# When the sample attention's keys are loaded and its first steps start, in a one-layer hybrid decoder step

## The chip, the cores and the metric

The kernel runs on one core of a Trainium2 chip. The metric is the device time in microseconds of one execution, lower is better. Before the change it was 835.45 us, the median of three executions (833.49 to 836.05).

## The reference

One decoder layer is computed for two groups of tokens with the same weights: a prompt of 256 tokens and 8 sample sequences of 8 tokens, whose keys and values of 256 past tokens lie in a paged cache. Cut to what matters:

```python
h = rmsnorm(x, norm1_g)
proj = h @ w_in                        # 12 sections; the attention takes fq, fk, fv and the gates ff
h_a = mlstm_sequence(q_a, k_a, v_a, ig, lf_a, C, n, m)      # matrix memory, one branch
q_b, k_b = rmsnorm(fq, q_norm_g), rmsnorm(fk, k_norm_g)     # per head of 128
k_all = concatenate([k_past, k_b]); v_all = concatenate([v_past, fv])
F_all = cumsum(concatenate([lf_past, lf_b]))
s = q_b @ k_all.T / sqrt(128) + F_q - F_k                   # causal
o_b = softmax(s) @ v_all                                    # forgetting attention, other branch
x = x + (sigmoid(ga) * (h_a @ w_branch_mlstm) + sigmoid(gb) * (o_b @ w_branch_fox)) @ w_out
x = x + hierarchical_moe(rmsnorm(x, norm2_g), ...)          # 32 experts, top 1 group, top 2 in it
```

For the samples b = 0 to 7 the attention has 8 heads, 8 queries and 256 past plus 8 new keys each.

## The kernel before

The dense weights come in 48 chunks of 256 columns, four for each of the twelve sections (mo, mk, mq, mv, ga, gb, fk, fq, fv, bm, bf, out). SyncE (SP) loads a chunk of 1 MB, ScalarE (ACT) rounds it to a high part (L829) and VectorE (DVE) subtracts to get the low part (L1172), and TensorE (PE) multiplies it in two or three units. In sections such as fv, units 0 and 1 are the two prompt tiles of 128 tokens and unit 2 the 64 sample tokens (L1811, 16 matmuls); unit 2 is evacuated by an ACT copy (L849) and a DVE addition (L1534, semaphore low_added). In bm a chunk has two units of 24 matmuls (L1821). Unit (fv,3,2) is unit 2 of chunk 3 of fv, the last of that section.

Between units every engine runs small stages in an order fixed by the function stages(): each entry names a unit behind which the stages stand, and each engine walks the same table in order and takes the stages that it has work for. Engines wait for each other only through semaphores, and each runs its own instructions strictly in that order.

For the samples a pipeline of stages runs, one step n after each unit from (fv,2,2), step 0, over (fv,3,1), step 1, (fv,3,2), step 2, and (bm,0,0), step 3, to step 9. For sample b:

- FS0(b), on DVE only: three copies (L1466, L1467, L1471) lay the new keys, the queries and the past forget values where PE reads them, then semaphore fs_ready. In step b-1; FS0(0) stands alone, behind unit (fv,2,1).
- FS1(b), in step b: PE waits for fs_ready and for the past keys (keys_landed) and computes scores (L2032, L2037, L2040). DVE takes the maximum (L1478 to L1480), ACT the exponential (L1041), DVE normalises.
- FS2(b), in step b+1: PE transposes the probabilities (L2049) and DVE lays them out (L1497, L1498).
- FS3(b), in step b+2: PE multiplies by the values: 24 matmuls of 128x128, 48 records in the trace (L2067), in three groups j: j = 0 and 1 are the two pages of past values, j = 2 the new ones, which lie in fv. In FS3(0) alone PE waits, ahead of group j = 2, until all of fv is evacuated.
- FS4(b), also in step b+2: a transpose into the output of the attention.

In each step PE runs FS3, FS2, FS1, then stages FP3, FP2, FP1 of the prompt's attention (L2013 is in FP2), then FS4.

GpSimd (POOL) issues the loads of past keys and values on its own queue, in a fixed order. Each sample needs two DMAs of 512 KB for keys (L664) and two for values (L679), and each time it first reads two page numbers. keys(b) goes to a first buffer for b = 0 and odd b, to a second for b = 2, 4, 6; the second lies on an area that PE reads as the dense input up to unit (fv,3,1) (unit (fv,3,2) reads another copy of the samples' part). keys(2) waits until that unit is done; the others wait until PE is past FS1(b-2), keys(1) past FS1(0). values(b) has two buffers in turn and waits from b = 2 on until PE is past FS3(b-2). The order of issue is values 0, keys 1, values 1, keys 2, keys 3, values 2, keys 4, the two stores of the new v rows (L641), values 3, keys 5, values 4, keys 6, values 5, keys 7, values 6, values 7.

After the attention come the sections bm, bf and out, the router, and the 32 experts, whose 96 MB of weights SP streams through buffers as they come free; the first wait of that stream behind the router is for its split input.

Of the kernel before, what the change touches and what calls it, by code (L numbers as in the profile page):

```python
# [30 lines left out]
TP, BS, TS = 256, 8, 8  # L31
# [6 lines left out]
HF, DF = 8, 128  # L38
# [10 lines left out]
CPS = D // CW  # L49
# [18 lines left out]
def units_of(c):  # L68

    return 2 if SECTIONS[c // CPS] in BY_FEATURE else 3  # L70


def stages():

    order = [(c, u) for c in range(NCH) for u in range(units_of(c))]
    at = {cu: [] for cu in order}

    def after(section, chunk, unit, n=0):

        return at[order[order.index((CPS * SECTIONS.index(section) + chunk, unit)) + n]]  # L80

    for n in range(1, 6):
        after("mo", 0, 1, 1 + 3 * (n - 1)).append(("G", n, 0))
    for t in range(3):
        after("mq", 1 + t, 1).append(("KT", t, 0))

    for h in range(HM):
        after("mv", h, 2, 2 if h < HM - 1 else 1).append(("P2", 0, h))
        after("mv", h, 2).append(("P1", 0, h))
    after("ga", 0, 0).append(("F1", 0, 0))  # L90
    for h in range(HM):
        after("ga", 1, 1, h).append(("P2", 1, h))
        after("ga", 0, 1, h).append(("P1", 1, h))
    after("ga", 0, 1).append(("F3", 0, 0))
    after("ga", 1, 0).append(("F2", 0, 0))

    after("ga", 2, 1).append(("SA", 0, 0))
    after("ga", 3, 0).append(("F1", 1, 0))
    for h in range(HM):
        for b in range(BS):  # L100
            line = after("ga", 3, 1, (h * BS + b) * 9 // (HM * BS))
            line.append(("SB", h, b))
            if h == 0 and b in (4, 5, 6):
                line.extend({4: (("F2H", 1, 0),), 5: (("F2L", 1, 0), ("F2H", 1, 1)), 6: (("F2L", 1, 1),)}[b])
        if h < HM - 1:
            line.append(("SA", h + 1, 0))
    after("ga", 3, 1).append(("F3", 1, 0))
    after("fk", 0, 0).append(("F1", 2, 0))
    after("fk", 0, 1).append(("F3", 2, 0))
    after("fk", 1, 0).append(("F2", 2, 0))  # L110

    for w, section in enumerate(("fk", "fq")):
        for t in range(3):
            after(section, 3, 2, 2 * t).append(("N1", w, t))
            after(section, 3, 2, 2 * t + 3).append(("N2", w, t))

    after("fv", 2, 1).append(("FS0", 0, 0))
    for n in range(HF + 2):
        line = after("fv", 3, 0, n) if n else after("fv", 2, 2)
        line.extend((k, n - s, 0) for s, k in ((2, "FS3"), (1, "FS2"), (0, "FS1"), (-1, "FS0")) if 0 <= n - s < BS)  # L120
        line.extend((k, n - s, 0) for s, k in ((2, "FP3"), (1, "FP2"), (0, "FP1")) if 0 <= n - s < HF)
        if n >= 2:
            line.append(("FS4", n - 2, 0))
    return at
# [32 lines left out]
def hybrid_step(nc, A, O):  # L157

    AT = stages()
    fill, count = {}, {b: 0 for b in range(8)}  # L160
    for c in range(NCH):
# [6 lines left out]
    with ctx:  # L168
        handles = {}

        def sem(name):
            if name not in handles:
                
                handles[name] = ctx.enter_context(nc.semaphore(name))
            return handles[name]
# [22 lines left out]
        def take(n):  # L198
            top[0] += n
            assert top[0] <= FW, top[0]  # L200
            return fm[:, top[0] - n:top[0]]

        def cube(ap, a):
            return ap.rearrange("p (a b) -> p a b", a=a)
# [5 lines left out]
        upto, last, maskT, mask, after = take(128), take(128), take(128), take(128), take(128)  # L210
# [62 lines left out]
        fv = cube(take(3 * D), 3)  # L273
# [116 lines left out]
        def keys_of(b):  # L390

            return KTc[1 if b >= 2 and b % 2 == 0 else 0]

        def keys_landed(b):

            other = b >= 2 and b % 2 == 0
            return sem("other_keys_in" if other else "keys_in"), 16 * NPAGES * (b // 2 if other else BS + 1 + (b + 1) // 2)

        def of_head(ap, h):

            n = HF // 2
            at = DIAGQ * n * (h // n) + HQ * (h % n)
            return ap[:, at:at + HQ]

        def units(c):

            return sum(units_of(k) for k in range(c)), units_of(c)

        def n_low(c):

            return sum(units_of(k) == 3 for k in range(c))
# [5 lines left out]
        def first(section):  # L417

            return CPS * SECTIONS.index(section)
# [157 lines left out]
        def _(pool):  # L577
# [57 lines left out]
            def pe_past(st):  # L635

                b = banks_of(st)[-1]
                pool.wait_ge(sem(f"bank_full{b}"), fill[st, b] + 1)

            def out(dst, src, name):  # L640
                pool.dma_start(dst, src).then_inc(sem(name), 16)  # L641
# [10 lines left out]
            def pages(b):  # L652

                return [pool.value_load(pt[0:1, b * NPAGES + j:b * NPAGES + j + 1], min_val=0, max_val=NPHYS - 1)
                        for j in range(NPAGES)]

            def keys(b):

                if b == 2:
                    pool.wait_ge(sem("unit_full"), units(first("bm"))[0] - 1)  # L660
                elif b:
                    pe_past(("FS1", max(b - 2, 0), 0))
                for j, page in enumerate(pages(b)):
                    pool.dma_start(keys_of(b)[:, :, j * PAGE:(j + 1) * PAGE],  # L664
                                   A["cache_kT"][bass.ds(page, 1)].rearrange("a d h s -> (a d) h s"))\
                        .then_inc(keys_landed(b)[0], 16)
# [7 lines left out]
            def values(b):  # L674

                if b >= 2:
                    pe_past(("FS3", b - 2, 0))
                for j, page in enumerate(pages(b)):
                    pool.dma_start(Vc[b % 2][:, j, :], A["cache_v"][bass.ds(page, 1)].rearrange("a s f -> (a s) f"))\  # L679
                        .then_inc(sem(f"values_in{b % 2}"), 16)  # L680
# [28 lines left out]
            g(nc.gpsimd.memset(qms, 0.0))  # L709
            g(nc.gpsimd.memset(Ps[0:NS, :], 0.0), sem("att_zeroed"))  # L710
            values(0)
            keys(1)
            values(1)
            keys(2)
            keys(3)
            for b in range(2, BS):
                if b == 3:

                    pool.wait_ge(sem("unit_free_a"), units(first("bm"))[0] - n_low(first("bm")))
                    pool.wait_ge(sem("low_added"), n_low(first("bm")))  # L720
                    out(O["v_prompt"], fv[:, 0:2, :], "v_stored")
                    out(O["v_sample"], fv[0:NS, 2, :], "v_stored")
                values(b)
                if b + 2 < BS:
                    keys(b + 2)

            pool.wait_ge(sem("o_split"), KC)
            g(nc.gpsimd.iota(iota, pattern=[[1, SLOTS]], base=0, channel_multiplier=0,
# [79 lines left out]
        def _(act):  # L808
# [108 lines left out]
            def P1(st):  # L917
                _, c, h = st
                n = c * HM + h
                if n == 0:  # L920
                    act.wait_ge(sem("gate_acts"), 2)
                if n >= 2:
                    pe_past(("P2", (n - 2) // HM, (n - 2) % HM))
                s(A_(kw[n % 2], kM(c, h), ACT.Copy, scale=ew[:, c, 8 + h:9 + h]), sem("kw_ready"))
# [848 lines left out]
        def _(pe):  # L1773
# [3 lines left out]
            def claim(st, b):  # L1777

                if fill[st, b]:
                    pe.wait_ge(sem(f"bank_free{b}"), fill[st, b])  # L1780

            def full(ins, b):
                ins.then_inc(sem(f"bank_full{b}"), 1)
# [268 lines left out]

            def FS3(st):
                b = st[1]
                pe.wait_ge(sem("fs_pt"), b + 1)
                pe.wait_ge(sem(f"values_in{b % 2}"), 16 * NPAGES * (b // 2 + 1))
                claim(st, 4)
                for j in range(3):
                    if b == 0 and j == 2:

                        pe.wait_ge(sem("unit_free_a"), units(first("fv") + CPS)[0] - n_low(first("fv") + CPS))
                        pe.wait_ge(sem("low_added"), n_low(first("fv") + CPS))
                    for h in range(HF // 2):
                        for i in range(2):
                            g = h + HF // 2 * i
                            w = slice(DF * g, DF * (g + 1))
                            ins = mm(bank[4][HQ * i:HQ * (i + 1), 0:DF], of_head(PTm[:, j, :], g),  # L2067
                                     Vc[b % 2][:, j, w] if j < 2 else fv[:, 2, w],
                                     start=(h == 0 and j == 0), stop=(h == HF // 2 - 1 and j == 2),
                                     skip_group_check=True)  # L2070
                full(ins, 4)
# [265 lines left out]
```

## Time and profile before

| | |
|---|---|
| median of 3 executions | 835.45 us (833.49 to 836.05) |
| profiled execution, its own time | 833.49 us |
| its span | 832.0 us |
| PE busy | 739.5 us, 89% |
| DVE busy | 401.7 us, 48% |
| ACT busy | 298.4 us, 36% |
| POOL busy | 140.0 us, 17% |
| read / written | 184.24 MB / 23.12 MB |

The span is the time from the first to the last instruction of the profile; the execution's own time is 1.5 us longer. PE is the tensor engine's matmuls and PEld its weight loads. An fp32 matmul shows as two records. A line of a timeline gives the start in us from the span's start, the duration, the engine, the line of the kernel, the operation with its output and inputs, and in brackets how long the engine was idle ahead of it and who released it; "issue" means that the profile shows no instruction as the releaser, and a wait for a load appears so. DMAs issued by POOL are timed at the issue; the time to landing is given apart.

### The profile page before, as it was taken

Reading aid. Unit: us, or ns where it says so; the run is one execution under the profiler, and the core shown is the slowest. Engines: PE = TensorE matmul, PEld = TensorE weight load, DVE = VectorE, ACT = ScalarE, POOL = GpSimd, SP = SyncE. Lnnn points to the kernel's source line nnn. Section 1 sums busy time; section 2 is a strip of 40 time slices with the busy share of each in tenths; the row PEclk is TensorE's granted clock in tenths of the full one; section 3 lists DMA queues with packets and bytes.
Section 4 is the critical chain, followed back from the end, with each engine's and each line's share of the span. In section 5 each row is a group of like instructions: output and inputs, shape, how many; then the busy total and the mean of one; then the engine's idle time right before and its main releaser. Section 6 shows DMA issues by size and latency. Waiting matters only on the chain.

```text
span 832.0 us, 14577 instructions
## 1 busy us (share of the span) xinstructions
PE 739.5 (89%) x5478; PEld 592.1 (71%) x5478; DVE 401.7 (48%) x939; ACT 298.4 (36%) x550; POOL 140.0 (17%) x247
## 2 busy tenths in 40 slices
PE   2999999999999999999899999895899999778770
PEld 1899999998666698998678889884665555344430
DVE  3466233465755556575566657755732222121123
ACT  5532644374543354555322234545221111111110
POOL 5001000001444200232312101000012222211210
PEclk9999999999999999999999999997899999999995
DMA  5344333224888643636776337965599999999985
GB/s 193 102 153 147 139 127 132 102 102 163 256 254 243 214 148 113 216 111 216 239 262 231 110 117 294 343 269 215 224 415 416 419 418 418 419 420 418 420 338 201
DMA packets 38186, 202.58 MB, mean 243 GB/s; under 512 B 7442, under 2 KB 7970, under 8 KB 18914
## 3 DMA queue, kind: packets, MB, share of 16 engines
q1 hardware_dynamic: 23938, 158.98, 49.4%
q0 software_dynamic: 13744, 41.32, 15.6%
q10 hardware_dynamic: 432, 1.31, 0.4%
q8 instruction: 46, 0.75, 0.4%
q14 instruction: 26, 0.21, 0.1%
HBM read 184.24 MB, written 23.12 MB: 249 GB/s over the span
## 4 chain that ended last, share of the span: by engine, by line
PE 64%; DMA 16%; DVE 10%; ACT 5%; issue 4%; SPq 0%; DVEq 0%; ACTq 0%; POOLq 0%
PE bank L1821 22%; PE bank L1825 12%; DMA fm<-in_w_moe 10%; PE bank L2183 7%; PE bank L1811 4%; DMA em<-in_w_moe 3%; PE bank L2203 3%; PE bank L1983 3%; DVE rm L1172 2%; ACT rm L829 2%; PE bank L2155 2%; PE bank L1972 2%; PE bank L2067 1%; DMA fm<-y_rows 1%; PE bank L2032 1%
## 5 line engine op out<-in xcount | busy, mean ns | idle before, releaser
L1821 PE MATMUL bank<-rm 128*128 128x320 f32 x1344 | 207.3, 313 | 1.6 <-ACT fm L857 1.6
L1821 PEld LDWEIGHTS bank<-rm 128*128 128x128 f32 x1344 | 198.9, 189 | 5.7 <-issue 3.1
L1172 DVE TENSOR_TENSOR rm<-fm,rm 128x2048 fp32r<-128x2048 f32 x48 | 110.0, 2292 | 72.1 <-ACT rm L829 71.5
L1825 PE MATMUL bank<-rm 128*128 128x256 f32 x960 | 123.8, 289 | 2.4 <-DVE fm L1563 2.4
L1825 PEld LDWEIGHTS bank<-rm 128*128 128x128 f32 x960 | 119.9, 196 | 3.3 <-issue 2.9
L2183 PE MATMUL bank<-fm,em 128*64 128x256 f32 x368 | 90.9, 392 | 16.6 <-DMA fm<-in_w_moe 11.2
L829 ACT ACTIVATE rm<-fm 128x2048 fp32r<-128x2048 f32 x48 | 91.9, 1915 | 17.1 <-PE bank L1821 10.9
L2183 PEld LDWEIGHTS bank<-fm,em 128*64 128x64 f32 x368 | 48.6, 140 | 51.6 <-issue 29.6
L2185 PE MATMUL bank<-fm,em 128*64 128x256 f32 x320 | 76.9, 384 | 0.0
L1130 ACT ACTIVATE fm<-bank 64x256 f32<-64x256 f32 x32 | 12.0, 376 | 137.5 <-PE bank L2185 137.5
L761 POOL DMA_INDIRECT y_rows<-fm,im x32 | 28.9, 903 | 166.5 <-DVE fm L1718 166.5
L2185 PE MATMUL bank<-em 128*64 128x256 f32 x192 | 50.6, 411 | 0.0
L684 POOL DMA_DIRECT2D fm<-in_state_C x32 | 17.6, 550 | 164.6 <-DVE fm L1325 119.4
L1811 PE MATMUL bank<-rm 128*128 128x256 f32 x320 | 42.9, 287 | 0.0
L1404 DVE SCALAR_TENSOR_TENSOR fm<-fm,bank 128x257 f32<-128x257 f32 x64 | 28.0, 479 | 30.2 <-PE bank L1983 30.0
L1723 DVE TENSOR_TENSOR fm<-bank,fm 64x256 f32<-64x256 f32 x32 | 13.6, 426 | 59.9 <-ACT fm L1130 59.8
L1739 DVE COPY fm<-bank 128x128 f32<-128x128 f32 x32 | 9.3, 291 | 66.6 <-PE bank L2194 66.5
L2185 PEld LDWEIGHTS bank<-fm,em 128*64 128x64 f32 x320 | 41.3, 137 | 0.0
L2183 PE MATMUL bank<-em 128*64 128x256 f32 x144 | 36.0, 395 | 5.8 <-DMA em<-in_w_moe 5.8
L1811 PEld LDWEIGHTS bank<-rm 128*128 128x128 f32 x320 | 40.0, 192 | 1.6 <-DVE fm L1563 1.5
L2203 PE MATMUL bank<-em,fm 128*64 128x512 f32 x144 | 34.0, 593 | 1.5 <-issue 0.9
L1718 DVE COPY fm<-bank 64x512 f32<-64x512 f32 x32 | 22.2, 694 | 26.9 <-PE bank L2203 26.8
(399 smaller groups left out, 986.1 us busy)
## 6 DMA issues: line engine op xcount, KB each, us to landing
fm<-in_w_moe SPq DMA_DIRECT2D x57, 1024.0 KB, 23.2
fm<-in_w_dense SPq DMA_DIRECT2D x48, 1024.0 KB, 4.9
em<-in_w_moe SPq DMA_DIRECT2D x39, 1024.0 KB, 27.1
fm<-in_state_C POOLq DMA_DIRECT2D x32, 257.0 KB, 5.4
out_C_sample<-fm POOLq DMA_DIRECT2D x32, 257.0 KB, 6.5
fm<-in_cache_v POOLq DMA_DIRECT2D x16, 512.0 KB, 4.9
fm<-in_cache_kT POOLq DMA_DIRECT2D x10, 512.0 KB, 7.5
em<-in_cache_kT POOLq DMA_DIRECT2D x6, 512.0 KB, 6.0
```

The costliest lines, as they stand in the source:

```text
L761: pool.indirect_dma_start(y_rows, bass.IndirectOffsetOnAxis(ap=row_i[:, v:v + 1].bitcast(U32), axis=0), yrow[v % NY], None, bounds_check=6 ...
L829: s(A_(pair[c % 2][0], cube(raw[c % RAW1], KC), ACT.Copy), sem("hi_done"))
L1172: s(TT(pair[c % 2][1], cube(raw[c % RAW1], KC), pair[c % 2][0], ALU.subtract), sem("split_done"))
L1404: done(STT(Cout[n % NCOUT][:, k, :], Cin[n % NCIN][:, k, :], dec8[:, HM * b + h:HM * b + h + 1], bank[bk][:, 0:DE], ALU.mult, ALU.add), bk)
L1718: CP(yrow[v % NY][:, D // 2:D], bank[4 + v % 2][CAP:2 * CAP, :]).then_inc(sem("e_y_right"), 1)
L1811: ins = mm(bank[b][:, 0:CW], samp[:, k, :], w[:, k, :], start=(k == 0 and i == 0), stop=(k == KC - 1 and i == 1))
L1821: ins = mm(bank[b][:, 0:NT], w[:, k, P * u:P * (u + 1)], a[:, k, :], start=first, stop=final)
L1825: ins = mm(bank[b][0:r, 0:CW], a[:, k, TILE0[u]:TILE0[u] + r], w[:, k, :], start=first, stop=final)
L1983: full(mm(bank[bk][:, 0:DE], kwm[n % 2][rows, 0:P], vx2[rows, h, :], start=True, stop=True), bk)
L2183: last_g = mm(bank[b][0:CAP, 0:FE], x[:, k, :], g[:, k, :], start=(k == 0), stop=(k == KC - 1), skip_group_check=True)
L2185: last_u = mm(bank[b][CAP:2 * CAP, 0:FE], x[:, k, :], u[:, k, :], start=(k == 0), stop=(k == KC - 1), skip_group_check=True)
L2203: ins = mm(bank[b][CAP * j:CAP * (j + 1), :], hT[:, k, :], w[:, k, 512 * j:512 * (j + 1)], start=(k == 0), stop=(k == 1), skip_group_check ...
```

## The change

There are three edits.

1. In stages(), FS0(0) stands behind unit (fv,2,2) instead of (fv,2,1). It is now the first stage of step 0, behind DVE's evacuation of that unit.
2. On POOL, the order of issue becomes values 0, keys 1, values 1, keys 2, values 2, the two stores of v, keys 3, values 3, keys 4, values 4 and so on to keys 7, values 7: each sample's keys right ahead of its values. keys(2) waits for the last unit of fv instead of the last but one. The buffers and the other waits stay.
3. On PE, FS3(0) waits for all of fv ahead of its first matmul instead of ahead of group j = 2, and the loops over heads h and groups j change places in FS3 of all samples, with the same matmuls.

```diff
--- before.py
+++ after.py
@@ -114,7 +114,7 @@
             after(section, 3, 2, 2 * t).append(("N1", w, t))
             after(section, 3, 2, 2 * t + 3).append(("N2", w, t))
 
-    after("fv", 2, 1).append(("FS0", 0, 0))
+    after("fv", 2, 2).append(("FS0", 0, 0))
     for n in range(HF + 2):
         line = after("fv", 3, 0, n) if n else after("fv", 2, 2)
         line.extend((k, n - s, 0) for s, k in ((2, "FS3"), (1, "FS2"), (0, "FS1"), (-1, "FS0")) if 0 <= n - s < BS)
@@ -657,7 +657,7 @@
             def keys(b):
 
                 if b == 2:
-                    pool.wait_ge(sem("unit_full"), units(first("bm"))[0] - 1)
+                    pool.wait_ge(sem("unit_full"), units(first("bm"))[0])
                 elif b:
                     pe_past(("FS1", max(b - 2, 0), 0))
                 for j, page in enumerate(pages(b)):
@@ -709,20 +709,15 @@
             g(nc.gpsimd.memset(qms, 0.0))
             g(nc.gpsimd.memset(Ps[0:NS, :], 0.0), sem("att_zeroed"))
             values(0)
-            keys(1)
-            values(1)
-            keys(2)
-            keys(3)
-            for b in range(2, BS):
+            for b in range(1, BS):
                 if b == 3:
 
                     pool.wait_ge(sem("unit_free_a"), units(first("bm"))[0] - n_low(first("bm")))
                     pool.wait_ge(sem("low_added"), n_low(first("bm")))
                     out(O["v_prompt"], fv[:, 0:2, :], "v_stored")
                     out(O["v_sample"], fv[0:NS, 2, :], "v_stored")
+                keys(b)
                 values(b)
-                if b + 2 < BS:
-                    keys(b + 2)
 
             pool.wait_ge(sem("o_split"), KC)
             g(nc.gpsimd.iota(iota, pattern=[[1, SLOTS]], base=0, channel_multiplier=0,
@@ -2052,15 +2047,15 @@
 
             def FS3(st):
                 b = st[1]
+                if b == 0:
+
+                    pe.wait_ge(sem("unit_free_a"), units(first("fv") + CPS)[0] - n_low(first("fv") + CPS))
+                    pe.wait_ge(sem("low_added"), n_low(first("fv") + CPS))
                 pe.wait_ge(sem("fs_pt"), b + 1)
                 pe.wait_ge(sem(f"values_in{b % 2}"), 16 * NPAGES * (b // 2 + 1))
                 claim(st, 4)
-                for j in range(3):
-                    if b == 0 and j == 2:
-
-                        pe.wait_ge(sem("unit_free_a"), units(first("fv") + CPS)[0] - n_low(first("fv") + CPS))
-                        pe.wait_ge(sem("low_added"), n_low(first("fv") + CPS))
-                    for h in range(HF // 2):
+                for h in range(HF // 2):
+                    for j in range(3):
                         for i in range(2):
                             g = h + HF // 2 * i
                             w = slice(DF * g, DF * (g + 1))
```

## Rows read from the trace of the kernel before

**Rows 1.** The page, busy us (share of the span) and instructions of each engine.
```profile
PE 739.5 (89%) x5478; PEld 592.1 (71%) x5478; DVE 401.7 (48%) x939; ACT 298.4 (36%) x550; POOL 140.0 (17%) x247
```

**Rows 2.** Chain of waits, 380 to 410 us: start us, duration us, what.
```profile
386.93 1.28 ACT L1041
...
396.19 2.30 DVE rm L1172
```

**Rows 3.** Timeline of PE: start us, us, engine line operation, count [idle before <-releaser].
```profile
383.15 1.97 PE L2032 MATMUL bank<-fm 128*32 128x264 f32 x16
...
387.31 6.00 PE L1825 MATMUL bank<-rm 128*128 128x256 f32 x48
...
395.09 1.97 PE L2032 MATMUL bank<-fm 128*32 128x264 f32 x16 [1.46 <-issue]
...
401.20 2.15 PE L1811 MATMUL bank<-rm 128*128 128x256 f32 x16
...
407.67 1.07 PE L2067 MATMUL bank<-fm 128*32 128x128 f32 x16 [1.68 <-DVE fm L1534]
...
408.99 1.97 PE L2032 MATMUL bank<-em,fm 128*32 128x264 f32 x16
...
421.31 1.98 PE L2032 MATMUL bank<-fm 128*32 128x264 f32 x16
...
425.80 0.52 PE L2013 MATMUL bank<-fm 128*128 128x128 f32 x3 [0.97 <-DVE fm L1498]
...
457.80 2.81 PE L2067 MATMUL bank<-fm 128*32 128x128 f32 x48
...
473.16 1.97 PE L2032 MATMUL bank<-fm 128*32 128x264 f32 x16
```

**Rows 4.** Timeline of DVE around FS0(0) and the evacuation of unit (fv,2,2).
```profile
381.31 0.19 DVE L1466 COPY fm<-fm 128x64 f32<-128x64 f32 x1
...
381.77 0.23 DVE L1471 COPY fm<-fm 128x128 f32<-128x128 f32 x1
383.79 0.42 DVE L1534 TENSOR_TENSOR fm<-bank,fm 64x256 f32<-64x256 f32 x1 [1.79 <-ACT fm L849]
```

**Rows 5.** Timeline of POOL: loads of keys and values, stores of v.
```profile
389.66 0.95 POOL L664 DMA_DIRECT2D fm<-in_cache_kT  x1 [1.16 <-issue]
...
395.06 1.79 POOL L664 DMA_DIRECT2D em<-in_cache_kT  x2 [2.54 <-issue]
...
410.81 1.15 POOL L679 DMA_DIRECT2D fm<-in_cache_v  x2 [9.55 <-issue]
413.44 1.79 POOL L664 DMA_DIRECT2D em<-in_cache_kT  x2 [1.47 <-issue]
415.22 0.57 POOL L641 DMA_DIRECT2D out_v_prompt<-fm  x1
...
462.39 1.15 POOL L679 DMA_DIRECT2D fm<-in_cache_v  x2 [8.98 <-issue]
```

**Rows 6.** Landing: all loads of line 664, then those issued from 399 to 403.
```profile
DMA to landing us min/median/max: 5.2/6.6/8.8
...
fm<-in_cache_kT POOLq DMA_DIRECT2D x2, 512.0 KB, 8.3
```

**Rows 7.** PE behind a gap; then busy time by stretch (PE, PEld, DVE, ACT, POOL, PEclk, DMA share, GB/s).
```profile
89.94 1.30 PE L1821 MATMUL bank<-rm 128*128 128x320 f32 x6 [1.58 <-ACT fm L857]
...
91.00:94.00 3.00, 3.00 (x13) 3.00 (x13) 1.59 (x1) 1.74 (x2) 0.00 (x0) 0.50 0.00 0
...
401.00:414.55 13.55, 11.17 (x122) 9.22 (x120) 6.20 (x28) 3.73 (x16) 2.48 (x5) 1.00 0.63 207
```

**Rows 8.** Busy time by stretch around the start of the expert weights' stream.
```profile
580.00:600.00 20.00, 16.59 (x100) 13.41 (x100) 15.91 (x40) 5.39 (x10) 1.23 (x2) 0.77 0.52 195
...
582.00:587.00 5.00, 3.10 (x12) 2.85 (x13) 4.68 (x10) 0.00 (x0) 0.00 (x0) 0.50 0.00 0
...
600.00:640.00 40.00, 39.40 (x287) 23.29 (x288) 14.77 (x39) 6.96 (x15) 7.69 (x10) 1.00 1.01 416
```

## The prediction

> **What bounds the kernel now.** I read the page first: the tensor engine (PE) is busy 89% of the span [rows 1], so a microsecond of PE idle time is dear unless something else sets that stretch. Then the chain of waits over the stretch that the edit touches, 380 to 480 us. From 386 to 407 us the chain runs through VectorE (DVE) and ScalarE (ACT), not PE: the exponential's table load and a weight split stand in it [rows 2]. So in steps 0 to 2 of the sample attention, PE waits on DVE, and what matters is when PE hands FS1(0) to DVE and when DVE hands the last value columns back. Then PE's timeline [rows 3], DVE's [rows 4] and GpSimd's (POOL) [rows 5], to see how long before its use each load of keys is issued, and how long loads take to land [rows 6].
>
> **Edit 1: FS0(0) one unit later.** FS0(0) is three DVE copies. Now they run from 381.31 to 382.00, beside PE's matmuls, and FS1(0) starts at 383.15 the moment PE gets there [rows 3, 4]. After the edit they stand behind the evacuation of unit (fv,2,2), whose last operation on DVE ends at 383.79 + 0.42 = 384.21. Three copies with gaps are 0.69, so they end at 384.93, and PE starts FS1(0) at about 385.0 instead of 383.15: +1.85. Nothing hides it: the chain enters DVE right behind FS1(0) [rows 2]. The first load of keys(1), released by FS1(0), moves along with it; PE's wait for it (1.46 us, at 395.09) lies beside the DVE chain and costs nothing on its own. Everything up to 407.67, where PE is released by the last value columns [rows 3], slides by 1.85.
>
> **Edit 2: FS3(0) waits for the value columns before its first matmul.** Now 32 of its 48 records run before that wait. All 48 take 2.81 us in step 6, the 16 behind the wait 1.07 [rows 3]. So 2.81 - 1.07 = 1.74 us leave the cover of the wait and stand behind it: +1.74. The wait's release is not later for it, since DVE needs nothing of FS3(0) before. Queued behind the waiting instruction are FS2(1), FS1(2) and PE's whole next unit. The loops' new order (h outside, j inside) issues the same 48 records with the same tiles. I take 0. Their spacing is now (2.81 - 1.07)/32 = 54.4 ns, and 128 columns at 2.4 GHz are 53.3, so at most 8 x 48 x 1.1 ns = 0.4 us could be gained; I allow as much for a loss.
>
> **Edit 3: the loads of keys are issued later.** keys(2) is released by the last unit of fv, not the last but one. Now it is issued at 395.06, 1.75 us after the unit that ends at 387.31 + 6.00 = 393.31, for a use at 408.99: 14 us ahead. After: the unit of 401.20 + 2.15 = 403.35 ends at 405.20 (with edit 1), the first DMA starts 1.8 later at 407.0, the second 0.9 later at 407.9 [rows 3, 5]. Landing: the second of keys(1) started at 389.66 and PE went on at 395.09, 5.4 us. The extremes of all sixteen are 5.2 and 8.8, and 8.3 is the median of keys(3), which had two other transfers ahead of it [rows 6]. keys(2) now has the queue to itself, so I take 5.4 to 6.5: landed at 413.3 to 414.4. PE, with edits 1 and 2, would reach FS1(2) at 408.99 + 1.85 + 1.74 = 412.6. The wait is 0.7 to 1.8, I take 1.1.
> The Trainium skill (DMA: Bandwidth & Descriptors, section on the SWDGE path) fits one such DMA as 2.0 us plus bytes at 436 per ns; for the 1 MB pair that would be an estimate of 4.4 us and no wait at all. The trace's 5.4 is for the same transfer and decides.
> keys(3) to keys(7) now stand behind values(b-1), which waits for FS3(b-3). For b = 3: values(2) is issued 2.07 us after FS3(0) ends (408.74 to 410.81), takes 1.15, then come the two stores of v (2 x 0.57) and two page reads (1.5, as between 411.96, the end of values(2), and 413.44), then two DMAs 0.9 apart (1.79 for two): the second starts 6.7 us after FS3(0)'s end. With 1.25 MB of stores ahead of it I take 7.4 to land: 14.1 us. FS1(3) now starts 421.31 - 408.74 = 12.6 after FS3(0); with step 2's added wait (1.1 to 1.7) 14.0, and 0.97 us of PE's wait for DVE at 425.80 can take up more. I put 0.5 on it, between 0 (landing 6.6) and 1.5 (landing 8.8). For b = 7: FS3(4) ends at 457.80 + 2.81 = 460.61, values(6) go out at 462.39, the second DMA of keys(7) at 465.9, landed with the median 6.6 at 472.5, and the need is at 473.16 [rows 3, 5, 6]. So 0.7 us spare; b = 4 to 6 follow the same pattern. I take 0 for b = 4 to 7. Key loads move past values and the stores only; SP's queue is not touched; it waits for the stores of v only in chunk 3 of bf, more than a section later.
>
> **The clock.** PE's idle time in step 2 becomes one gap: from 403.35 to 407.67 it had the 32 other records of FS3(0) in it, and now it is empty, 4.3 us. In this trace a gap of 1.58 before 89.94 was followed by a granted clock of 0.50 (1.2 GHz) from 91 to 94 with PE fully busy, while 1.68 here was not (1.00 over 401 to 414.55, 2.4 GHz) [rows 7]. So I expect the clock to fall around FS3(0). A fall as long as the one at 91 to 94, 3 us or a little more, takes half of its length, up to 1.7 us, from FS3(0) and FS2(1) [rows 7], side by side with the landing of keys(2): together they cost the later of the two, 1.7 instead of 1.1.
> The Trainium skill (TensorE: Matmul & The Clock Gate, section on the HAM clock gate) has half rate as the resting state that activity lifts; by that alone the short gap at FS1(0) is harmless, by the trace's 1.58 it may not be.
> A fall there would slow FS1(0) itself, on the chain, by up to 1.7; I leave it to the range.
>
> **Sum.** 1.85 + 1.74 + 1.7 + 0.5 = 5.8 us. Does it reach the end? From 600 us the DMA engines are saturated (share 1.01, 416 GB/s), but just ahead, 582 to 587, they move nothing and wait for the router's result [rows 8], which hangs on PE and DVE. So the weight stream starts 5.8 later and ends 5.8 later. The profiled execution took 833.49 (span 832.0 and 1.5 around it), so it gives 839.3; the median of the runs shown, 835.45, is 1.96 above the profiled one, so the forecast in its terms is 841.2.
>
> **Rivals.**
> Keys late in every step (0.10). The spare time of b = 4 to 7 is under 1 us at the median landing; at the 8.8 us seen once, keys(7) lands at 474.7, 1.5 late. Five such steps are 7.5: 835.45 + 5.3 + 7.5 = 848.3. For it speaks that values and keys now go out back to back; against it the median of 6.6.
> Step 2's load and clock both hidden (0.12): the clock stays up and keys(2) land in under 4.7. Only edits 1 and 2 remain: 3.6, so 839.0.
> Not slower, by the router's clock (0.09). Between 580 and 600 the granted clock is 0.77 [rows 8], so for 46% of 20 us, 9.2 us, PE works at 1.2 GHz, and it is on the path for most of them. Whether it falls there hangs on how PE's short waits ahead of it lie in time, and these all move. Kept up, it gives back up to 4.6: 841.2 - 4.6 = 836.6, no change, and 834.4 with the case before. Against it: the waits are the router's own and stay as long. It decides if the clock stays at 1.00 there.
> The end takes it up (0.06): if the expert weights were already flowing without a break when the delay arrives, 835.5. Against it are the 5 us at 0.00 share.
> The forecast keeps 0.63, with its own range 838.5 to 843.5.
>
> **Range and chances.** 837.0 to 846.0 leaves out about 0.10 above and 0.08 below. Such a kernel's measurement can't tell less than about 0.3% (2.5 us) from nothing. Forecast, late keys and the hidden case are all over that: slower 0.85. The other two hold 0.15: same 0.11, faster 0.04 (the router's clock together with hidden loads).
>
> **What would show it.** FS1(0) on PE starting about 1.8 later than DVE allowed before, with PE idle ahead of it, and released by DVE's third copy; one gap of some 4.3 us ahead of 48 records of FS3(0) in one piece; a lower granted clock right behind; a short wait of FS1(2) for a DMA; the second DMA of keys(b) starting 5 to 7 us after FS3(b-3). The forecast is wrong if FS1(3) to FS1(7) each wait for a DMA, or if PE reaches the unit (bm,0,0) less than 3 us later than now, or if the stretch from there to the end has another length.

## The result, and the profile after

The changed kernel took 844.9 us in the median of four runs (843.1 to 845.64), the kernel before 834.47 beside it. The ratio is 1.012, with a 95% interval of 1.0094 to 1.0148: about 10 us slower. The forecast was 841.2, in a range of 837.0 to 846.0. The profiled execution took 841.31 us, 7.8 more than the profiled one of before. Medians here leave out one execution of the kernel "order only" below, at 864.62 us, whose granted clock was 0.843 where its others had 0.965 to 0.972.

PE's timeline of the changed kernel, with the columns of [rows 3] (its lines are numbered 5 lower, and FS1 is L2027, FS3 L2062):
```profile
381.28 2.08 PE L1806 MATMUL bank<-rm 128*128 128x256 f32 x16
385.12 1.98 PE L2027 MATMUL bank<-fm 128*32 128x264 f32 x16 [1.76 <-DVE fm L1466]
...
397.45 1.98 PE L2027 MATMUL bank<-fm 128*32 128x264 f32 x16 [1.86 <-issue]
...
403.17 2.15 PE L1806 MATMUL bank<-rm 128*128 128x256 f32 x16
409.84 4.48 PE L2062 MATMUL bank<-fm 128*32 128x128 f32 x48 [4.52 <-DVE fm L1529]
...
414.57 1.97 PE L2027 MATMUL bank<-em,fm 128*32 128x264 f32 x16
...
429.60 1.98 PE L2027 MATMUL bank<-fm 128*32 128x264 f32 x16 [2.65 <-DMA fm<-in_cache_kT]
...
480.32 1.97 PE L2027 MATMUL bank<-fm 128*32 128x264 f32 x16
```
The reader is to see four places. PE idles 1.76 us ahead of FS1(0), released by DVE's third copy. Ahead of FS3(0) there is one gap of 4.52, and then its 48 records take 4.48 instead of 2.81. FS1(2), at 414.57, waits for nothing. FS1(3) waits 2.65 for keys(3), where it waited for nothing in [rows 3]. The granted clock fell at FS3(0) (columns as in [rows 7]):
```profile
405.00:409.00 4.00, 0.31 (x3) 0.11 (x1) 2.45 (x10) 1.47 (x5) 1.79 (x2) 1.00 0.08 13
409.00:412.00 3.00, 2.16 (x27) 2.19 (x29) 0.70 (x2) 0.00 (x0) 0.00 (x0) 0.74 0.94 284
```

Where a profile's early stages ran a little faster or slower, everything behind is shifted. So I count from the start of PE's unit (fv,2,2), the row at 381.28, and compare with before, where that unit started here:
```profile
381.14 2.08 PE L1811 MATMUL bank<-rm 128*128 128x256 f32 x16
```
FS1(0) at 385.12 - 381.28 = 3.84 against 383.15 - 381.14 = 2.01 is +1.83. The same sum gives +5.44 at FS1(2), +8.15 at FS1(3) and +7.02 at FS1(7); from there to the end it is +0.5.

The chain of waits of the changed kernel in steps 2 and 3 (start us, duration us, what):
```profile
409.32 0.43 DVE fm L1529
409.75 0.09 issue
409.84 4.50 PE bank L2062 x48
414.36 0.29 POOLq L654
...
416.69 0.54 POOL fm L679
417.23 0.54 POOL out_v_prompt L641
...
420.07 0.85 issue
420.93 8.58 DMA fm<-in_cache_kT
429.51 0.09 issue
429.60 1.98 PE bank L2027 x16
```
This is the new wait in one view: FS3(0) releases values(2), the stores of v follow, then keys(3), and FS1(3) waits for their landing. In the kernel before, nothing of POOL's queue stands in this chain from 380 to 430 us.

### The profile page after: what moved, and what is told of

The parts are those of the page before. It is cut to its first block, busy times and chain, and to the rows that moved or that the text cites. A ratio compares the mean times of both kernels' runs of the same rounds, so it can differ in the third digit from the quotient of the medians.

```text
span 839.7 us, 14577 instructions
## 1 busy us (share of the span) xinstructions
PE 737.7 (88%) x5478; PEld 589.1 (70%) x5478; DVE 403.3 (48%) x939; ACT 298.4 (36%) x550; POOL 140.2 (17%) x247
## 4 chain that ended last, share of the span: by engine, by line
PE 59%; DMA 17%; DVE 12%; ACT 5%; issue 5%; POOLq 0%; POOL 0%; SPq 0%; DVEq 0%; ACTq 0%
PE bank L1816 21%; DMA fm<-in_w_moe 10%; PE bank L1820 9%; PE bank L2178 7%; DMA em<-in_w_moe 3%; PE bank L1806 3%; PE bank L2198 3%; DVE rm L1167 3%; PE bank L1978 2%; ACT rm L824 2%; PE bank L2062 2%; PE bank L1967 1%; PE bank L2150 1%; DMA fm<-in_cache_kT 1%; DMA fm<-y_rows 1%
## 5 line engine op out<-in xcount | busy, mean ns | idle before, releaser
L1816 PEld LDWEIGHTS bank<-rm 128*128 128x128 f32 x1344 | 197.4, 188 | 7.0 <-issue 3.1
L1820 PE MATMUL bank<-rm 128*128 128x256 f32 x960 | 120.8, 284 | 2.4 <-DVE fm L1558 2.4
L1820 PEld LDWEIGHTS bank<-rm 128*128 128x128 f32 x960 | 116.9, 191 | 3.3 <-issue 2.9
L2178 PE MATMUL bank<-fm,em 128*64 128x256 f32 x368 | 92.6, 397 | 18.1 <-DMA fm<-in_w_moe 12.8
L2178 PEld LDWEIGHTS bank<-fm,em 128*64 128x64 f32 x368 | 49.2, 141 | 53.8 <-issue 31.5
L2180 PE MATMUL bank<-fm,em 128*64 128x256 f32 x320 | 81.4, 401 | 0.0
L2180 PE MATMUL bank<-em 128*64 128x256 f32 x192 | 46.3, 384 | 0.0
L2180 PEld LDWEIGHTS bank<-fm,em 128*64 128x64 f32 x320 | 43.0, 142 | 0.0
L1806 PE MATMUL bank<-rm 128*128 128x256 f32 x320 | 42.9, 286 | 0.0
L1806 PEld LDWEIGHTS bank<-rm 128*128 128x128 f32 x320 | 40.0, 191 | 1.6 <-DVE fm L1558 1.0
L2178 PE MATMUL bank<-em 128*64 128x256 f32 x144 | 34.6, 383 | 4.3 <-DMA em<-in_w_moe 4.3
```

The source lines that it names most:

```text
L1806: ins = mm(bank[b][:, 0:CW], samp[:, k, :], w[:, k, :], start=(k == 0 and i == 0), stop=(k == KC - 1 and i == 1))
L1816: ins = mm(bank[b][:, 0:NT], w[:, k, P * u:P * (u + 1)], a[:, k, :], start=first, stop=final)
L1820: ins = mm(bank[b][0:r, 0:CW], a[:, k, TILE0[u]:TILE0[u] + r], w[:, k, :], start=first, stop=final)
L2178: last_g = mm(bank[b][0:CAP, 0:FE], x[:, k, :], g[:, k, :], start=(k == 0), stop=(k == KC - 1), skip_group_check=True)
L2180: last_u = mm(bank[b][CAP:2 * CAP, 0:FE], x[:, k, :], u[:, k, :], start=(k == 0), stop=(k == KC - 1), skip_group_check=True)
```

## The experiments

Edits are numbered as in the prediction: 1 moves FS0(0), 2 is FS3(0)'s wait and loop order, 3 the loads of keys (2 and 3 stand the other way round in the list of the change). Each was compared with the kernel before in the same batch. "From the unit" means the count just explained, always against the one profile of before. Behind FS1(7) the other profiles took from 0.7 us less to 1.9 us more than it, most of them 0.2 to 1.4 more. There is one profile for each row, and where the clock falls differs between executions, so differences of some 2 us between rows can be the clock's.

| | ratio (95% interval) | FS1(0) | FS1(2) | FS1(3) | FS1(7) |
|---|---|---|---|---|---|
| changed kernel | 1.012 (1.0094 to 1.0148) | +1.83 | +5.44 | +8.15 | +7.02 |
| the same again | 1.0128 (1.011 to 1.0146) | +1.83 | +5.99 | +9.10 | +9.60 |
| edit 1 alone | 1.0012 (0.999 to 1.0034) | +1.83 | +1.81 | +1.82 | +1.78 |
| edit 2 alone | 1.0058 (1.0041 to 1.0074) | -0.01 | +2.96 | +2.96 | +2.95 |
| edit 3 alone | 1.0057 (1.004 to 1.0074) | 0.00 | +2.81 | +5.20 | +5.75 |
| stores behind keys(3) | 1.0075 (1.0045 to 1.0104) | +1.83 | +5.45 | +5.45 | +5.44 |
| old order of issue | 1.0062 (1.0037 to 1.0086) | +1.83 | +5.45 | +5.44 | +5.46 |
| busy gap | 1.0081 (1.0052 to 1.011) | +1.83 | +4.59 | +6.75 | +5.63 |
| table early | 0.999 (0.9975 to 1.0006) | 0.00 | -1.26 | -1.26 | -1.26 |
| late release only | 1.0054 (1.0034 to 1.0075) | -0.01 | +2.80 | +4.37 | +4.37 |
| order only | 1.003 (1.0011 to 1.0048) | 0.00 | 0.00 | +3.36 | +2.26 |
| columns early | 0.9947 (0.9929 to 0.9966) | -0.01 | -1.23 | -1.23 | -1.23 |
| split too | 0.9966 (0.9952 to 0.998) | 0.00 | -3.07 | -3.08 | -3.09 |

**Edit 1 alone.**
```diff
-    after("fv", 2, 1).append(("FS0", 0, 0))
+    after("fv", 2, 2).append(("FS0", 0, 0))
```


> Edit 1 alone: FS0(0) behind unit (fv,2,2), all else as before. Theory A (three prices on one path, each read from its own gap): PE idle some 1.8 us ahead of FS1(0), nothing given back later, no key load waits at step 2 or 3, so +1.9 to +2.1 us over before. Theory B (the late start is taken up again by PE's waits for VectorE in steps 1 and 2, which were there before): the waits at 399 and 407 us shrink by as much, and the time is within 0.5 us of before.

836.36 against 835.65 us. The +1.83 at FS1(0) is still there at FS1(7). Theory B falls in the profile: the wait for DVE ahead of the last 16 records of FS3(0) keeps its 1.68 [rows 3], since the whole chain moved. The one ahead of FP2(0) shrank from 1.63 to 1.08, but the wait for keys(1) ahead of it grew by as much, from 1.46 to 2.02. The runs without a profile show about 1 us, and their interval holds both 0 and 1.8.

**Edit 2 alone.** The two waits of FS3(0) stand ahead of its first matmul and the loops over h and j change places, as in the change.


> Edit 2 alone: FS3(0) waits ahead of its first matmul, and the loops of FS3 change places. Theory A: one empty gap of 4.3 us ahead of FS3(0), then 48 records in one piece; if the granted clock falls behind the gap they take some 4.5 us, as in the changed kernel, and the kernel takes +3.4; if it stays at full they take 2.8, and it is +1.7. Theory B (the loop order itself slows FS3): the later FS3(1) to FS3(7) take more than 2.81 us each.

839.68 us. PE around FS3(0) in this kernel, and the busy time of its surroundings (columns as in [rows 7]):
```profile
402.83 1.06 PE L2005 MATMUL bank<-fm 128*128 128x256 f32 x2
...
409.26 4.09 PE L2067 MATMUL bank<-fm 128*32 128x128 f32 x48 [2.63 <-issue]
...
422.85 2.81 PE L2067 MATMUL bank<-fm 128*32 128x128 f32 x48
```
```profile
403.00:404.00 1.00, 1.00 (x6) 0.82 (x4) 0.69 (x3) 0.68 (x4) 0.00 (x0) 0.50 0.99 410
...
408.00:412.00 4.00, 2.74 (x28) 2.76 (x30) 1.06 (x3) 0.14 (x1) 0.00 (x0) 0.57 0.12 31
412.00:416.00 4.00, 4.00 (x56) 2.86 (x53) 1.01 (x6) 0.00 (x0) 0.56 (x1) 1.00 0.01 2
```
The clock fell and the 48 records took 4.09 us. It had fallen once already, ahead of unit (fv,3,2): L2005 took 1.06 at 402.83, where it takes 0.59 at the full clock. So that unit ended later and the gap was 2.63 instead of the expected 4.3. The first fall cost nothing, for it lay beside the wait for the value columns, which were ready no later (FS3(0) started 26.47 after unit (fv,2,2), where the wait ended at 26.53 before). FS3(1) took 2.81 as before, so the loop order costs nothing, and theory B falls. The price is 1.74 for the order of waiting, less 0.06, and 4.09 - 2.81 = 1.28 for the second fall: +2.95, between theory A's two values.

**Edit 3 alone.** Release of keys(2) and order of issue as in the change, stages() and FS3 as before.


> Edit 3 alone: keys(2) waits for the last unit of fv, and each sample's keys go out right ahead of its values. Theory A: with FS1(2) back at 409 us the load of keys(2) is no longer hidden: second DMA at about 406, landed at 411.2 to 411.6, so PE waits some 2.4 us at FS1(2), and 0 to 1 at FS1(3); b = 4 to 7 don't wait. +2.4 to +3.5 us. Theory C (the runs without a profile lost 3 us more than the profiled one because later key loads miss their use in some executions): the timed runs stand more than 1.5 us above what the profile of this kernel shows, and a wait for a load shows at some b of 4 to 7.

840.66 us. FS1(2) of this kernel:
```profile
415.28 3.73 PE L2027 MATMUL bank<-em,fm 128*32 128x264 f32 x16 [2.49 <-issue]
```
The wait of 2.49 for keys(2) is as expected, but the clock fell during it (0.50 from 414 to 420), and FS1(2)'s first 16 records took 3.73 instead of 1.97 [rows 3]. From FS1(2) to FS1(3), with no wait between them, that takes 2.39 more. With a wait of 0.60 at FS1(4) it makes +5.75, well over the expected 2.4 to 3.5. Theory C fails in its main part: the median of the timed runs is below the profiled execution's 842.91. The wait at one b of 4 to 7 that it asked for did come, at FS1(4), but it is short.

**The changed kernel again.**


> The changed kernel unaltered, once more. Theory A: FS1(0) +2.0, FS3(0) +3.4, FS1(3) +1.5 again, +7.1 at unit (bm,0,1), and the timed runs +7 to +8. Theory C: the first two come again within 0.3 us, but the waits at FS1(3) to FS1(7) differ from the first profile, and the timed runs are at +10 again. Theory D (what differs between executions is the clock in the router's stretch): the distance from unit (bm,0,1) to the end differs by over 1 us between the two profiles.

845.67 us. PE at FS3(0) and FS1(3), then busy time around both:
```profile
410.64 5.03 PE L2062 MATMUL bank<-fm 128*32 128x128 f32 x48 [4.53 <-DVE fm L1529]
...
431.36 2.86 PE L2027 MATMUL bank<-fm 128*32 128x264 f32 x16 [3.05 <-DMA fm<-in_cache_kT]
```
```profile
408.00:412.00 4.00, 1.35 (x14) 1.39 (x16) 1.49 (x4) 1.20 (x5) 1.68 (x2) 0.55 0.58 155
412.00:416.00 4.00, 4.00 (x43) 3.71 (x41) 0.22 (x1) 0.00 (x0) 0.00 (x0) 0.60 0.38 112
432.00:436.00 4.00, 4.00 (x30) 3.04 (x27) 1.19 (x8) 0.00 (x0) 1.79 (x2) 0.57 0.95 362
```
The 1.83 came again to the digit. What differs between two executions of one program is the clock: here it fell already in the gap and stayed low through nearly all of FS3(0), and it fell a second time behind the wait at FS1(3). There the first profile got 1.1 us back, and this one lost 0.5 more. The timed runs of both batches (+10) agree with this profile's +9.6 and not with the first one's +7.0. Theory C's later waits did not show (none at FS1(4) to FS1(7)), and theory D's distance from there to the end differs by 0.5 us between the two profiles, not by over 1. That most timed executions had both falls is an inference, for they have no trace. Their mean granted clocks, 0.961 to 0.967 in the first batch and 0.964 to 0.970 in this one, lie between the two profiles' 0.972 and 0.961, most of them nearer the lower, and do not tell where the clock fell.

**Stores behind keys(3).**
```diff
-                if b == 3:
-                    ...
-                    out(O["v_prompt"], fv[:, 0:2, :], "v_stored")
-                    out(O["v_sample"], fv[0:NS, 2, :], "v_stored")
                 keys(b)
+                if b == 3:
+                    ...
+                    out(O["v_prompt"], fv[:, 0:2, :], "v_stored")
+                    out(O["v_sample"], fv[0:NS, 2, :], "v_stored")
                 values(b)
```


> The changed kernel with the two stores of v issued behind keys(3) instead of ahead of it. Counted from the unit (fv,2,2), the changed kernel stood 5.4 and 6.0 us over before at FS1(2) in its two profiles and 8.2 and 9.1 at FS1(3). Theory A (keys(3) land late because 1.25 MB of stores and 1.1 us of their issue stand ahead of them in POOL's queue): the second DMA of keys(3) starts 1.1 us sooner after FS3(0) and lands in under 7.5 us, and the wait at FS1(3) falls from 2.7 to 3.1 us to under 1; +5.5 to +6.5 at FS1(7). Theory B (they land late because of what else the DMA engines carry, values(2) above all, whatever the order): landing stays at 8 us or over and the wait only falls by the 1.1 us of issue, to 1.6 to 2.0.

840.22 against 834.83 us. The landing of keys(3) in the changed kernel:
```profile
fm<-in_cache_kT POOLq DMA_DIRECT2D x2, 512.0 KB, 8.2
```
and in this one, without the stores ahead:
```profile
fm<-in_cache_kT POOLq DMA_DIRECT2D x2, 512.0 KB, 6.0
```
Then FS1(3) here:
```profile
426.74 1.98 PE L2027 MATMUL bank<-fm 128*32 128x264 f32 x16
```
No wait at all, and +5.44 at FS1(7). Theory A holds: the 1.25 MB of stores ahead in the queue made keys(3) late, by their issue (1.1 us) and by 2.2 us of landing.

**Old order of issue**, with edits 1 and 2 and the late release of keys(2):
```diff
-            for b in range(1, BS):
+            keys(1)
+            values(1)
+            keys(2)
+            keys(3)
+            for b in range(2, BS):
                 ...
-                keys(b)
                 values(b)
+                if b + 2 < BS:
+                    keys(b + 2)
```


> Edits 1 and 2 and the later release of keys(2), with the order of issue of the kernel before (keys(3) right behind keys(2), ahead of values(2)). Theory A (all that the changed kernel loses from FS1(3) on comes from the order): FS1(2) at +5.4 to +6.0 from unit (fv,2,2) as in the changed kernel, no wait for a load at FS1(3), and +5.4 to +6.0 still at FS1(7). Theory B (keys(3), issued with keys(2), now slow its landing): FS1(2) waits for its load, over +6.5 there.

840.19 us, +5.46 at FS1(7) from another direction. All that the changed kernel loses from FS1(3) on comes from the order. Theory B falls: FS1(2) is at the same +5.45.

**Busy gap.**
```diff
-                if b == 0:
-                    ...
                 ...
                 claim(st, 4)
+                if b == 0:
+                    for n in range(24):
+                        mm(bank[4][HQ * (n % 2):HQ * (n % 2 + 1), 0:DF], of_head(PTm[:, n % 3 % 2, :], n % 4 + 4 * (n % 2)),
+                           Vc[0][:, n % 2, 0:DF], start=True, stop=True, skip_group_check=True)
+                    pe.wait_ge(sem("unit_free_a"), units(first("fv") + CPS)[0] - n_low(first("fv") + CPS))
+                    pe.wait_ge(sem("low_added"), n_low(first("fv") + CPS))
```


> The changed kernel with 24 more matmuls (48 records, their result is overwritten) in PE's gap ahead of FS3(0), so that PE is busy for some 2.8 of the 4.5 us. Theory A (FS3(0)'s 4.5 us are the granted clock's fall behind the gap): the clock stays at 1.00 from 405 to 416, FS3(0) takes 2.8 us, and FS1(2) is then held by the landing of keys(2) instead: +4.2 to +4.6 there from unit (fv,2,2), 1.0 to 1.5 less than in the changed kernel. Theory B (FS3(0) is slow for another reason, its first touch of the value columns or of a bank): it still takes over 4 us at a clock of 1.00.

The two waits for the value columns now stand behind the added matmuls. 841.36 us. PE, then its clock:
```profile
409.78 2.81 PE L2064 MATMUL bank<-fm 128*32 128x128 f32 x48 [1.06 <-DVE fm L1529]
413.61 1.98 PE L2027 MATMUL bank<-em,fm 128*32 128x264 f32 x16 [0.69 <-issue]
...
428.09 1.97 PE L2027 MATMUL bank<-fm 128*32 128x264 f32 x16 [2.11 <-issue]
```
```profile
404.00:420.00 16.00, 13.55 (x166) 11.80 (x165) 6.70 (x29) 3.06 (x12) 5.29 (x8) 1.00 0.50 148
```
With the gap filled the clock stays at 1.00 and FS3(0) takes 2.81 again, in this one profile, where all five profiles with the gap left empty have the fall; theory B falls. But FS1(2) now waits 0.69 for keys(2), which the slow FS3(0) had hidden, so only 0.85 us come back there: the two lie side by side, as forecast. keys(3) are late here too.

**Table early**, on the kernel before:
```diff
                 b = st[1]
+                if b == 0:
+                    s(A_(small[0:1, 95:96], small[0:1, 95:96], ACT.Exp))
                 act.wait_ge(sem("fs_max"), b + 1)
```


> The kernel before (no part of the change) with one exponential of a single element on ACT ahead of its wait in FS1(0), so that the table load of 1.28 us comes while ACT is idle. Theory A (steps 0 to 2 are bound by the chain through VectorE and ACT from the end of FS1(0) to the last value columns, which is why edit 1 passed through whole): FS1(0) at 0.0, FS1(2) to FS1(7) at -1.2 to -1.3 from unit (fv,2,2). Theory B (the load of keys(1) or PE itself would hold it anyway): under 0.5 us gained.

834.0 against 834.83 us. -1.26 at FS1(2), the table load's 1.28 [rows 2], though the wait at FS1(1) is still there (1.41). So the chain through DVE and ACT does bind these steps. Of the end it shows nothing: behind FS1(7) this profile took 1.85 us more than before, the most of all, and in the timed runs 1 us is inside the measurement's interval.

**Late release only.**
```diff
-                    pool.wait_ge(sem("unit_full"), units(first("bm"))[0] - 1)
+                    pool.wait_ge(sem("unit_full"), units(first("bm"))[0])
```


> Of edit 3 only the later release of keys(2); the order of issue stays as before, so keys(3) go out right behind keys(2). Edit 3 whole stood at +2.8 at FS1(2) and +5.2 to +5.8 from FS1(3) on. Theory A (release and order have a price each, the release at FS1(2), the order at FS1(3)): +2.5 to +2.8 at FS1(2), no wait for a load at FS1(3), and the same +2.8 at FS1(7), up to 1.7 more where the granted clock falls behind the wait. Theory B (a wait at FS1(2) is enough to unsettle what follows): over +5 at FS1(7) here too.

839.77 against 835.24 us. FS1(2):
```profile
412.46 3.56 PE L2032 MATMUL bank<-em,fm 128*32 128x264 f32 x16 [2.48 <-issue]
```
+2.80, then 1.57 more for the fall of the clock, +4.37 up to FS1(7): theory A with its addition. This one line costs 0.54%.

**Order only**, keys(2) released as before.


> Of edit 3 only the order of issue; keys(2) are released by the last unit of fv but one, as before. Theory A (the order's price is its own, keys(3) behind values(2) and the stores): 0 at FS1(2); the second DMA of keys(3) starts 6.6 us after FS3(0) ends, lands 8 us later, and FS1(3), 12.6 us after FS3(0), waits 1.8 to 2.4; up to 1.0 to 1.3 of it is taken up by PE's old wait ahead of FP2(2), so +1 to +1.5 at FS1(4) to FS1(7), or all of it where the clock falls. Theory B (the order costs only on top of the late release): no wait at FS1(3), within 0.5 us at FS1(7).

837.41 us. FS1(2) and FS1(3):
```profile
408.91 3.57 PE L2027 MATMUL bank<-em,fm 128*32 128x264 f32 x16
...
424.59 1.97 PE L2027 MATMUL bank<-fm 128*32 128x264 f32 x16 [1.61 <-issue]
```
The order has a price of its own: +3.36 at FS1(3), over the expected 1.8 to 2.4, and +2.26 at FS1(7). The landing of keys(3) was 8.4 in the median, and their first DMA started 6.06 after FS3(0)'s end, where it was 5.67 in the changed kernel. Only 1.61 of the 3.36 shows as a wait, because the clock fell at FS1(2) and PE came 1.75 later to FS1(3). The loads hang on FS3(0), which was over by then, so the fall lies beside the landing and, by these numbers, cost nothing of its own. The clock fell behind gaps of 0.69 and 1.68, the same that left it up in [rows 7].

**Columns early.** The version before, and unit (fv,3,2) evacuated inside FP1(1), on ACT ahead of its wait for the maximum and on DVE behind the maximum, instead of at its own place:
```diff
+                if h == 1:
+                    evac(first("fv") + 3, 2)
                 act.wait_ge(sem("fp_max"), h + 1)
...
                 s(TSC(small[:, 42:44], small[:, 40:42], -1.0, None, ALU.mult), sem("fp_max"))
+                if h == 1:
+                    evac(first("fv") + 3, 2)
                 dve.wait_ge(sem("fp_exp"), h + 1)
```


> A version meant to beat both: the kernel before with the table load early (as in the run before) and with the evacuation of unit (fv,3,2) moved on ACT and DVE into FP1(1), behind the maximum and ahead of the exponential, where DVE is idle for 1.3 us and ACT for 2.9. Theory A (the chain sets these steps and the value columns are its last link): FS3(0) needs no wait ahead of group j = 2; -1.3 from the table and -1.7 from the wait, about -3.0 at FS1(2) to FS1(7) from unit (fv,2,2). Theory B (once the columns come early, the load of keys(2) or FS2(1) holds FS1(2)): not more than -2.

831.8 us, 0.53% faster than before. FS3(0) needs no second wait (48 records in one piece). But in its profile the clock fell at FS1(1):
```profile
394.63 3.60 PE L2040 MATMUL bank<-fm 128*32 128x264 f32 x16 [1.63 <-issue]
...
404.08 2.81 PE L2075 MATMUL bank<-fm 128*32 128x128 f32 x48 [1.18 <-DVE fm L1449]
```
That leaves -1.23 in the profile, while the timed runs (-3.4 in the median, an interval of -2.8 to -5.9) agree with the -3 of theory A.

**Split too.** Also the split of the first bm chunk stands in FP1(0), on ACT ahead of the wait for the maximum, on DVE behind the maximum.


> The version before, and the split of the first bm chunk moved in step 0 from behind FP1(0) into the idle time around its exponential (2.3 us on DVE, 1.9 on ACT). Theory A: DVE reaches FS2(0) 2.3 us earlier, but FS1(1) is then held by the landing of keys(1), so the gain over the version before is 0.2 to 1.0 us: -3.2 to -4.0 at FS1(2). Theory B (the split is later than PE's unit (bm,0,0) needs it, or it delays the prompt's softmax): no gain or a loss.

832.9 us, 0.34% faster than before and not faster than the version without it (their intervals overlap). The profile has -3.09 at FS1(7), with the clock at 1.00 from 380 to 480 us. That is just short of theory A's -3.2 to -4.0, and the timed runs show no gain over the other version, as theory B had it. The profile of the version without it had lost some 1.6 us to the clock at FS1(1), so most of what lies between the two profiles is the clock and not the split.

## Why the prediction came out as it did

**FS0(0) later: right.** 1.85 was the price, 1.83 is measured, in every profile that has the edit. That nothing behind takes it up is shown by edit 1 alone; that the chain runs through DVE and ACT, by the early table.

**FS3(0) behind its wait, and the clock: right.** 1.74 and 1.7, together 3.44, against 5.44 - 1.83 = 3.61 and 5.99 - 1.83 = 4.16 in the two profiles. The gap was 4.5 where 4.3 was read off. The fall of the clock is shown by filling the gap. Its length was not right in every execution: taken as 3 us or a little more, it was nearly 7 in the second profile, and FS3(0) took 2.22 more there instead of 1.67.

**keys(2): hidden, as the sum had it.** The forecast said that its landing and the slow FS3(0) cost only the later of the two. In the changed kernel the wait is zero, though the prediction named a short one among its signs. Taken alone, the release costs 2.80.

**keys(3): the step that was mis-sized.** The prediction put 0.5 us on it, between 0 and 1.5. It is 8.15 - 5.44 = 2.71 and 9.10 - 5.99 = 3.11 at FS1(3), and net 1.6 and 3.6 at FS1(7): outside its bounds. Two entries were off. The landing was taken as 7.4; with the stores ahead in the queue it is 8.2. And the distance between FS3(0)'s end and the need was taken as 14.0, with step 2's delay of 1.1 to 1.7 in it. But that delay lay in FS3(0) itself, before its end, and behind the end PE had no wait for keys(2): the distance is the old 12.6. The start of the second DMA, 6.7 us after FS3(0), was right (414.32 to 420.9). 6.6 + 8.2 - 12.6 gives 2.2, plus the 0.4 us that the second DMA took beyond the mean.

**A second fall of the clock** was not in the sum: behind the wait for keys(3), in the second profile. It slowed the first 16 records of FS1(3) by 0.88 and kept PE from getting back the 1.3 us that the first profile regained between FS1(3) and FS1(4), where PE waits for DVE in [rows 3].

**keys(4) to keys(7): right**, no wait in either profile. Of the rivals, late keys in every step did not come, the hidden case neither; the clock in the router's stretch fell as before (0.61 over 22 us, from 570 to 592 before and from 575 to 597 in the changed kernel), and the end took nothing up: +7.02 at FS1(7) became +7.56 at the end.

The direction held and the range held the time, 3.7 us above the forecast. But the forecast's own range, 838.5 to 843.5, did not hold it, and none of the rivals accounts for the rest: it is keys(3) and the clock, each costing more than was put on it. By the second profile, which the timed runs agree with, +9.6 stands against the forecast's 5.8: 2.6 of the difference arises at FS1(3), 0.7 at FS3(0) and 0.5 behind FS1(3).

## What to carry to other kernels

Price a moved load from its release: the queue's work ahead of it, the two DMAs, and the landing with what is queued in front. Bulk stores that nobody waits for belong behind the loads that somebody does: moving two stores gave back what the new order had cost. Where the time to a later deadline is counted from some event, a delay lengthens it only if it lies behind that event; one that lies ahead of it, or is hidden beside another, must not be credited. And a wait on PE may cost more than itself, through the clock: 1.57 us more than its own 2.80 in the late release alone.

## What was not expected of the hardware

The clock's fall decides as much as the waits, and differs between executions of one program. Behind gaps of 1.63 and of 0.69 and 1.68 us it fell in two kernels (3.60 and 3.57 us for 16 records that take 1.97), and it stayed up behind such gaps in the kernel before (1.63, 0.70 and 1.68). Behind 0.91 and 2.18 in step 1 it fell in edit 2 alone and stayed up with the stores behind keys(3). In the gap ahead of FS3(0) or FS1(2), or right behind it, it fell in all seven profiles with 2.48 us or more there, but not behind the 2.65 at FS1(3) in the changed kernel's first profile. What sets this is not shown. Where nothing hid it, one fall cost 1.3 to 2.4 us of PE's time; in the changed kernel's second profile and in edit 3 alone the granted clock stayed at 0.50 for some 7 us.
